# State-space layer in chunks of four steps, computed inside the input product of the second block

## The reference, cut to what matters

```
h = rms_norm(x);  proj = h @ w_in            # 1024 -> 512 u, 3*1024 qkv, 8 f, 2*1024 gates
# 32 groups of 16 channels, 64 complex states each, one step size per group
lam  = exp(a*step);  xr + i xi = B' u_t      # B' folds (lam-1)/a into b
s_t  = lam * s_(t-1) + x_t                   # over the 512 tokens
y_t  = Re(C s_t) + d*u_t;  y = gelu(y)
val, gate = split(y @ w_glu);  y_ssm = val*sigmoid(gate)
y_att = forgetting_attention(q, k, v, f)
merged = sigmoid(g_ssm)*y_ssm + sigmoid(g_att)*y_att
x = x + merged @ w_out                       # then a product-key expert layer (PEER)
```

## Time and profile before

| | us |
|---|---|
| median of 3 runs (4550.99 to 4552.28) | 4551.06 |
| the profiled execution, its own time | 4546.91 |
| its span (first to last instruction) | 4545.2 |
| in it: ada stage, up to its last bias add | 112.0 |
| in-product of block 2, first product to the next stage's first DMA | 2051.9 to 2309.8 |
| state-space stage | 2435.7 to 2729.1 |
| gated product | 2729.1 to 2799.0 |
| share of the span: PE 85%, PEld 67%, DVE 61%, ACT 40%, POOL 7% | |

### The profile page before, as it was taken

The page is one execution under the profiler, slowest core; times in us unless marked ns, Lnnn a source line. Parts: engine busy times, 40 slices in busy tenths (PEclk is TensorE's granted clock), DMA queues, the critical chain, the costliest instruction groups (busy, mean ns, idle before and its releaser), DMA issues. The chain is left out here.

```text
span 4545.2 us, 49456 instructions
## 1 busy us (share of the span) xinstructions
PE 3885.0 (85%) x17136; PEld 3062.3 (67%) x17136; DVE 2775.7 (61%) x3805; ACT 1834.6 (40%) x1841; POOL 295.8 (7%) x405
## 2 busy tenths in 40 slices
PE   7878737999999999939974437799999999999999
PEld 3656536777777777727853115678888888888887
DVE  1333538999999999952237984267787643444443
ACT  0323315777777777722233003223444443222222
POOL 0012010000000000010024420000000000000000
PEclk9875858999999999969967668899999999999999
DMA  6200118999999999962200002234444445555554
GB/s 268 97 21 0 38 55 323 358 361 359 362 356 365 359 359 363 359 223 87 87 2 10 19 9 74 79 123 160 151 177 162 168 169 206 188 190 189 187 186 143
DMA packets 212075, 840.11 MB, mean 185 GB/s; under 512 B 18672, under 2 KB 84720, under 8 KB 134160
## 3 DMA queue, kind: packets, MB, share of 16 engines
q1 hardware_dynamic: 195024, 753.53, 45.9%
q10 hardware_dynamic: 9216, 58.72, 3.1%
q0 software_dynamic: 7712, 26.23, 1.8%
HBM read 741.91 MB, written 96.50 MB: 184 GB/s over the span
## 5 line engine op out<-in xcount | busy, mean ns | idle before, releaser
L1121 DVE TENSOR_TENSOR w_low<-w_raw,w_high 128x2048 fp32r<-128x2048 f32 x399 | 909.1, 2290 | 141.9 <-ACT w_high L1050 139.5
L1050 ACT ACTIVATE w_high<-w_raw 128x2048 fp32r<-128x2048 f32 x399 | 764.6, 1916 | 336.8 <-PE ps L122 189.8
L2006 DVE TENSOR_TENSOR uv_lo<-uv_raw,uv_hi 128x2048 fp32r<-128x2048 f32 x128 | 293.5, 2293 | 662.1 <-ACT uv_hi L1863 661.8
L120 PE MATMUL ps<-w_high,xT_high 128*128 128x512 f32 x1056 | 433.1, 410 | 20.5 <-issue 20.5
L121 PE MATMUL ps<-w_low,xT_high 128*128 128x512 f32 x1056 | 417.9, 396 | 0.0
L122 PE MATMUL ps<-w_high,xT_low 128*128 128x512 f32 x1056 | 417.7, 396 | 0.0
L120 PE MATMUL ps<-h4T_high,uv_hi 128*128 128x512 f32 x1024 | 410.3, 401 | 1.1 <-DVE uv_lo L2006 1.1
L120 PE MATMUL ps<-uv_hi,w_hi 128*128 128x512 f32 x1024 | 405.1, 396 | 2.6 <-issue 2.6
L121 PE MATMUL ps<-uv_lo,w_hi 128*128 128x512 f32 x1024 | 405.0, 396 | 0.0
L122 PE MATMUL ps<-uv_hi,w_lo 128*128 128x512 f32 x1024 | 405.0, 395 | 0.0
L122 PE MATMUL ps<-h4T_high,uv_lo 128*128 128x512 f32 x1024 | 399.4, 390 | 0.0
(11 more groups left out here) (452 smaller groups left out, 6895.1 us busy)
## 6 DMA issues: line engine op xcount, KB each, us to landing
w_raw<-in_w_gate_up SPq DMA_DIRECT2D x267, 1024.0 KB, 6.9
w_raw<-in_w_down SPq DMA_DIRECT2D x132, 1024.0 KB, 6.8
uv_raw<-in_peer_u SPq DMA_DIRECT2D x64, 1024.0 KB, 5.0
uv_raw<-in_peer_v SPq DMA_DIRECT2D x64, 1024.0 KB, 5.0
a_rows<-a_out SPq DMA_DIRECT2D x128, 256.0 KB, 2.1
g_rows<-spread ACTq DMA_DIRECT2D x16, 2048.0 KB, 6.4
qT<-g_rows SPq DMA_DIRECT2D x32, 1024.0 KB, 9.0
qT<-a_rows SPq DMA_DIRECT2D x64, 512.0 KB, 8.7
```

The source lines that it names most:

```text
L120: pe.matmul(out, l_hi, r_hi, start=first, stop=False)
L1050: act.activation(w_hi[:, n % SPLIT, :], w_raw[:, n % RAW, :], ACT.Copy).then_inc(s_wh, 1)
L1121: dve.tensor_tensor(w_lo[:, n % SPLIT, :], w_raw[:, n % RAW, :], w_hi[:, n % SPLIT, :].bitcast(F32), ALU.subtract).then_inc(s_wl, 1)
L2006: dve.tensor_tensor(uv_lo[:, n % 2, :], uv_raw[:, n % 2, :], uv_hi[:, n % 2, :].bitcast(F32), ALU.subtract).then_inc(s_lo, 1)
```

## The change

Four parts.

1. Tables in the first stage. The ada stage also loads the state-space parameters (behind the first `w_ada` tile; b and c as 1 MB, d as 64 KB), and VectorE makes from them powers of lambda, b and c times powers (`b_powers`, `c_powers`) and rotation tables for 128 chunks (`turns`). TensorE turns the b tables (32 transposes after tile 3) and makes the lag kernels (32 small matmuls after tile 6). SP stores the tables to DRAM at the end: d_b, d_c, d_turn with 2 MB each (d_c in 512-byte pieces), d_lag with 0.46 MB. The loops over tiles are written out; four banks instead of three; TensorE needs no bank count for the first four tiles.
2. Chunks of four. The 512 tokens are 128 chunks of 4. A pair of groups has 4*32 = 128 input rows (step, channel), one column per chunk; scans run over 128 columns instead of 512. What happens inside a chunk is one 128x128 matmul with the lag kernels. u is multiplied out with tokens of stride 4 as the stationary operand.
3. In-product in units. The `Gemm` is replaced by 53 units: u (4), f (1), gates (16), GLU (8), qkv (24). A unit holds a depth of 256 (512 KB; f is one unit), in a ring of 3. State-space pieces lie between units; tables come by POOL's DMA queue. Gates get their sigmoid when the bank is emptied. The GLU product reads y split in high and low.
4. The state-space and GLU stages are gone. The sum with the attention's result moves to the front of mix2 (`merge`), where TensorE starts its transposes when the first half of the columns is ready.

```diff
@@ first stage @@
+            sp.dma_start(wbuf[0], ...)                      # tile 0, then parameters
+            sp.dma_start(pc[A_RE], ...)   # A_IM, LS x2
+            sp.dma_start(bc_in[...], t["ssm_bc_2"]).then_inc(s_sin, 16)
+            sp.dma_start(d_in[:, :, :], t["ssm_d_2"]).then_inc(s_sin, 16)
+            for s in range(1, RING): ...                    # tiles 1, 2, then mod, x
+            for n in range(RING, 12):
+                sp.wait_ge(s_mm_a, n - RING + 1)
+                sp.dma_start(wbuf[n % RING], t["w_ada"][n, :, :])...
+            sp.wait_ge(s_blh, 8)
+            sp.dma_start(d_b..., b_turned...).then_inc(s_prep, 16)
+            for q in range(4): sp.dma_start(d_c[q, :, :]..., c_pow[...])...
+            sp.wait_ge(s_lagd, 1);  sp.dma_start(d_lag, lags...)
+            sp.wait_ge(s_rott, 1);  # two DMAs d_turn <- turn_t
+            sp.wait_ge(s_prep, 16 * 8)
@@ its VectorE order @@
+            b_powers(0); add_bias(0); b_powers(1); add_bias(1)
+            c_first(); c_powers(0); add_bias(2); c_powers(1); add_bias(3)
+            for k in range(8): powers(k)
+            add_bias(4)
+            for k in range(5): turns(k)
+            add_bias(5); turns(5); add_bias(6); turns(6); add_bias(7)
...
@@ its TensorE @@
+            for n in range(12):
+                pe.wait_ge(s_ld_a[n % RING], (n // RING + 1) * 16)
+                if n >= BANKS_A:
+                    pe.wait_ge(s_bank_a, n - BANKS_A + 1)
...
+                if n == 3:  # 8 x 4 transposes, each 4 wait s_lb 2 and s_blh
+                if n == 6:  # wait s_el 2; 16 pairs x 2 matmuls, N = 128
@@ in-product @@
+    DEEP, UK = 3, 2
+    CHUNKS = ["u", "f"] + ["g"] * 4 + ["z"] * 4 + ["p"] * 6
+    S0 = F_END + 2
+    INPUTS_AT = {F_END + 1: 0, S0 + 1: 1, S0 + 4: 2, S0 + 6: 3}
+    OUTPUTS_AT = {S0 + 3: 0, S0 + 6: 1, S0 + 8: 2, S0 + 11: 3}
...
+                if x >= DEEP:
+                    sp.wait_ge(s_low, x - DEEP + 1)          # SP: load unit x
...
+                        if kind == "u":
+                            l = [h[:, k, :].rearrange("p (c s) -> p s c", s=SUB)[:, m, :] for h in h3T]
...
+            for x in range(NU):                              # TensorE
+                unit(x)
+                if x == F_END: turn_u()                      # 16 transposes
+                if x in INPUTS_AT: inputs(INPUTS_AT[x])      # 8 matmuls N=128
+                if x - 1 in OUTPUTS_AT: turn_y(...)          # 4 transposes
+                if x in OUTPUTS_AT: outputs(OUTPUTS_AT[x])   # 12 matmuls N=128
...
+            for x in range(NU):                              # VectorE
+                if x + 2 < NU: low(x + 2)
+                if S0 <= x < S0 + 10:
+                    next(pieces[2 * (x - S0)]);  next(pieces[2 * (x - S0) + 1])
...
@@ mix2 @@
+    def merge(dve):
+        for c in range(2):
             for m in range(TT):
+                at = merged[:, m, c * CH:(c + 1) * CH]
+                dve_steps(dve.tensor_tensor(at, at, ug[:, m, D + c * CH:D + (c + 1) * CH], ALU.mult))
+                dve_steps(dve.tensor_tensor(at, at, ug[:, m, c * CH:(c + 1) * CH], ALU.add))
+            dve.sem_inc(s_mg, 1)
```

More of the change, by code:

```diff
@@ L221, in products, with turn @@
             self.each(pe, body)
-    def turn(pe, src, s_done, s_taken, kt=KT, banks=(4, 5), at=0):
+    def turn(pe, src, s_done, s_taken, kt=KT, banks=(4, 5), at=0, ready=None):
         for k in range(kt):
+            if ready is not None and k % 4 == 0:
+                pe.wait_ge(ready, k // 4 + 1)
             if k >= 2:
@@ L483, in _ @@
[L483 to L488, removed]
+            dve.wait_ge(s_pa, 1)
+            st(dve.tensor_tensor(pc[T1], pc[A_RE], pc[STEP], ALU.mult))
+            dve.sem_inc(s_pd, 1)
+            st(dve.tensor_tensor(pc[TH], pc[A_IM], pc[STEP], ALU.mult))
@@ new lines, in _ @@
+            for k in range(5):
+                turns(k)
+            add_bias(5)
+            dve.wait_ge(s_lbt, 8)
+            st(dve.memset(lags[:, :, 0:SUB - 1, :], 0.0))
+            turns(5)
+            add_bias(6)
+            turns(6)
+            dve.sem_inc(s_rott, 1)
+            add_bias(7)
+            dve.wait_ge(s_lagh, 4)
+            dve.tensor_tensor(lags[:, :, SUB - 1, :], lags[:, :, SUB - 1, :], d_in[:, :, :], ALU.add).then_inc(s_lagd, 1)
+            for n in range(8, 12):
+                add_bias(n)
@@ L1261, in emit @@
     gain3 = sb(stage, "gain3", [P, D])
[L1262 to L1267 removed]
+    DEEP, UK = 3, 2
+    w_raw = sb(stage, "win_raw", [P, DEEP, UK * CH])
@@ new lines, in emit @@
+    w_hi, w_lo = (sb(stage, f"win_{x}", [P, DEEP, UK * CH], F32R) for x in ("high", "low"))
+    yT_hi, yT_lo = (sb(stage, f"yT_{x}", [P, 4, SEQ], F32R) for x in ("high", "low"))
+    early, late = merged[:, 0:2, :].rearrange("p m d -> p (m d)"), merged[:, 2:4, :].rearrange("p m d -> p (m d)")
+    u_rows = early.rearrange("p (n s w) -> p n s w", n=PAIRS, s=SUB)
+    y_rows2 = early.rearrange("p (s d) -> p s d", s=SUB)
+    u_sub = late.rearrange("p (n k) -> p n k", n=PAIRS)
+    flat = qkv[:, :, :].rearrange("p m d -> p (m d)")
@@ new lines, in emit @@
+    NU = len(units)
+    last_of = {at: x for x, (at, *_, last) in enumerate(units) if last}
+    U_END, F_END, G0, Z0, Q0 = last_of[0], last_of[1], last_of[1] + 1, last_of[5] + 1, last_of[9] + 1
+    s_ss, s_sq, s_root, s_g, s_h, s_tp, s_tpe, s_tph = (
+        sem(f"norm3_{x}") for x in ("sums", "mean", "root", "gain", "h", "turned", "taken", "turned_high"))
+    s_wld = [sem(f"win_ld{s}") for s in range(DEEP)]
+    s_high, s_low, s_used, s_mm, s_bank = (sem(f"win_{x}") for x in ("split_high", "split_low", "used", "mm", "bank"))
@@ new lines, in emit, with wait_used @@
+    s_tb, s_tt, s_tc = ([sem(f"ssm_{x}_table{s}") for s in range(2)] for x in ("b", "turn", "c"))
+    s_u, s_uh, s_v, s_vu, s_z, s_y, s_yh, s_yt, s_yhi, s_ylo, s_gl = (
+        sem(f"ssm_{x}") for x in ("u_turned", "u_here", "inputs", "inputs_used", "states", "y", "y_here", "y_turned", "y_high", "y_low",
+                                  "gated"))
+    used_before = [sum(not u[-1] for u in units[:x + 1]) for x in range(NU)]
+    def wait_used(eng, x):
+        if units[x][-1]:
+            eng.wait_ge(s_mm, 4 * (units[x][0] + 1))
+        else:
+            eng.wait_ge(s_used, used_before[x])
```

737 lines of the change are left out of this document (464 added, 273 removed).

## The result

The changed kernel takes 4277.64 us (median of 4 runs, 4272.19 to 4278.32), the kernel before 4551.02 us beside it (median of 4). The ratio is 0.9401, 95% interval 0.9390 to 0.9412. The forecast was 4276, with a range of 4256 to 4312. The profiled execution took 4272.19 us; the forecast of that was 4272.3. That the two are so close is partly luck: single terms were off by up to 3.5 us, in both directions, and the profiled execution was the fastest of the four.

A forecast was written before the change was run, and what follows sets the result against it. VectorE was taken to bound the state-space stage, TensorE the in-product. Terms -363.3 + 69.9 + 9.8 + 9 = -274.6 from 4546.9 give 4272.3, plus 4.2 for the median: 4276 us, range 4256 to 4312.

The forecast's parts named there:

- What bounds what: VectorE sets the state-space stage's length, TensorE the in-product's; work moved there costs only what it costs TensorE.
- Stages removed, -363.3: State-space and GLU stages, from the first's first DMA to mix2's first DMA, drop out: -363.3 us.
- In-product, forecast +69.9: In-product stage grows by 43.5 + 25 + 3 - 2.0 + 0.4 = +69.9 us.
- The GLU's 192 products: In the in-product, 192 GLU matmuls of 512 columns at 0.2267 us each add +43.5 us.
- State space: TensorE's state-space passes and transposes in the in-product add +25 us, bounds 21 to 28.
- f in the middle, +3: In-product's f chunk behind u: following work starts at the low clock, +3 us, bounds -9 to +6.
- Strided loads, 0 taken: In-product, u's 96 stride-4 weight loads stay hidden, 0 us; rival at 0.44 adds 20 us, chance 0.10.
- Start, -2.0: In-product's start: VectorE splits two half-size units before turning to h, -2.0 us.
- What has to stay hidden: In-product: VectorE's 56 us fit beside 54 of products plus some 20 of passes; leak rival 4320, chance 0.14.
- mix2, +9.8: Front of mix2: 16 merges, 11.6 us, now precede the first `turned_low`, adding +9.8 us.
- First stage, forecast +9: First stage ends at 121 instead of 112 us, set by table stores: +9, bounds 0 to +20.
- The step from the profiled execution to the median: Whole kernel: the median of the runs lies 4.2 us above the profiled execution, added at the end.

The follow-up runs named there:

- experiment 2: Changed kernel without VectorE's state-space arithmetic inside the in-product, semaphores still raised at the same places: 4276.27 us.
- experiment 3: Changed kernel without any state-space work in the in-product (TensorE, ScalarE, VectorE, table loads); gated product reads the normed input instead: 4252.32 us.
- Experiment 1: Kernel before the change with its state-space and GLU stages left out, nothing else changed: 4182.7 us, ratio 0.9189.
- experiment 5: Changed kernel with the f chunk's operands swapped, 24 products of 512 columns plus four transposes in place of 96 of 8: 4260.51 us, ratio 0.9368.
- experiment 6: Changed kernel with the first stage's table stores moved to ScalarE's queue, each as soon as its table is done: 4271.73 us, ratio 0.9383.
- experiment 7: Changed kernel with the first stage's load of x moved behind that of tile 3: 4272.59 us, ratio 0.9388.
- 8: Changed kernel with mix2's first low parts of the turned operand made between the merges of the second half: 4273.42 us, ratio 0.9391.
- 10: Changed kernel with mix2's first four low parts between the merges and the first weight tile's split early: 4272.53 us, ratio 0.9397.
- experiment 9: Changed kernel with stationary tokens at stride four in f, q, k, v and stride two in the gates: 4285.33 us.
- experiment 4: Changed kernel with 9 of VectorE's 512-column instructions and 8 scans issued once more per state-space quarter: 4299.93 us.
- experiment 11: Changed kernel with f's operands swapped, table stores early, x behind tile 3, and mix2's merges woven with its first split early: 4250.32 us, ratio 0.9341.

## Why the prediction was right, step by step

- **What bounds what.** VectorE set the state-space stage and TensorE the in-product; work moved under TensorE then costs TensorE's part alone. Shown by experiments 2 (38.7 us of VectorE, no time) and 3.
- **Stages removed, -363.3.** Experiment 1 gave 363.6.
- **In-product, forecast +69.9, measured +67.6.** The GLU's 192 products at 0.2267 stand as forecast (43.5; 1184 to 1376 instructions, and no waits). State space: 25 forecast, 23.2 measured (experiment 3). Of these, 1.7 are there because u's transposes run at the low clock, which the forecast counts under f, so 21.5 stand against the 25. The pass was put too near its upper bound of 0.144, a row that holds the drain of a chain: 16 input passes took 1.70 us from start to start, 0.106 each.
  The parts as measured: 43.5 + 23.2 + 1.1 (restart behind f) + 0.7 (u's loads) - 2.7 + 1.4 (start) + 0.4 (end, taken over from the forecast and not measured) = 67.6; measured 67.6.
- **f in the middle, +3.** The chunk took 16.14 us, as before (16.1 by its starts), and the clock fell once, as forecast. The restart cost 1.1 (five products, 2.24 us in place of 1.13), the slower transposes 3.33 - 1.67 = 1.7 (experiment 5), 2.8 in all. Part of it is luck: in five other runs with this chunk unchanged (3, 6, 7, 8 and 10) the clock fell 2.8 to 3.0 us after its start and it took 17.65 to 17.8, while u had fewer products at the low clock. What I did not see is that the chunk's 16 us could be had for 5.5; it was read as a given.
- **Strided loads, 0 taken.** 0.7 measured; "a load of twice that still hides" was right but for 0.0083 each. The Trainium skill (SBUF — State Buffer, section "SBUF: two separate sides") says that each element at this stride touches a new 16-byte line; the bare load of 0.2335 against 0.111 agrees with its direction, and at stride 2, where two elements share a line, this case shows a price as well (0.0068), which the rule doesn't lead one to expect.
- **Start, -2.0.** The first product came 2.7 us earlier after the stage's first DMA (23.50 instead of 26.17), but 14 products ran at the low clock where it had been 7, which is 1.4 us back. That number varies from run to run with the same code ahead (7 in experiments 3 and 5, 1 in experiment 9).
- **What has to stay hidden.** Forecast was 56 us of VectorE against 54 of products and some 20 of passes; measured were 55.1 busy in 71. The Trainium skill (same page and section) has the rule that VectorE instructions of a two-port kind shut out GpSimd's writing of descriptors. This case shows no such effect: the tables' loads landed a median of 6.7 to 7.7 us after issue, and 6.5 to 8.1 in experiment 2, where VectorE does none of the state space; no TensorE wait names them.
- **mix2, +9.8.** From mix2's first DMA to the first split on VectorE it took 21.65 us, before 11.39: +10.3. From that DMA to the end of the program it was +8.8 in this execution; the seven others with the same code had +8.7 to +13.6.
- **First stage, forecast +9, measured +11.9.** The gap was where it should be (8.1 us for 6.7 forecast, tile 3 at 41.7 for 39), TensorE done at 118.2 for 117. The term that was mis-sized is the stores. They started 3 us sooner than forecast, at 98, but ended at 124 instead of 121: 26 us from first issue to the end, where 20 were forecast. The forecast reckoned with 2 MB in 4.9 us, 428 GB/s, and 2 us extra for the c powers in pieces of 512 bytes. From 98 to 122.5 us the DMA engines were busy nearly throughout (mean share 1.01, the last tile's load among it) but moved 349 GB/s. The four issues of the c powers also kept SP's queue for 14.9 us, and the turns were issued behind them at 115. No run changes the size of the pieces, so what this queue and what the slower transfer cost each isn't shown. Experiments 6 and 7 show the two halves of the stage: the stores set the end, and x in front of tile 3 the gap.

The mechanism held: what was removed, what was hidden and what TensorE paid came out as forecast. That the sum fits to 0.2 us is luck. The errors of +2.9 (first stage) and -2.3 (in-product), with +1.0 (attention), -0.8 (blocks between) and -1.0 (mix2), took each other away, in an execution whose first stage and whose end were among the shortest of those with the same code. The step from the profiled execution to the median was forecast as 4.2 us and was 5.5. The total should be read as right to some 3 us.

## What to carry to other kernels

Here the work of an engine with room cost nothing inside a stage that another engine fills, and some 20 us more of it would still have been covered. What decides is its busy time in the very stretch against the length of the stretch (here 55 in 71, with splits two units ahead), not the mean of the stage. When small pieces are moved, look at what they do to the clock of what follows, and at whether they must be small: swapping the stationary and the moving operand gave 14 us, where moving the chunk had cost 2.8. And a store whose results are needed much later can leave when its table is ready, on a queue that nothing urgent uses: that gave 3.6 us in experiment 6.

## What the hardware showed that was not expected

- Gaps cost more than their length here. Three waits of 17.9 us together lengthened a stage by 24.7 (experiment 4). After 8.1 to 8.3 us without work TensorE's next 16 products took 8.8 to 10.1 us in nine runs; after 3.0 us they took 7.13 in one run (experiment 7) and after 3.1 us 8.83 in another (experiment 11).
- The clock also fell under full load: 42 products of 8 columns ran 0.11 apart, then the granted clock went to 1.2 GHz and they were 0.21 apart, with no idle time between. In other runs of the same code it fell 26 to 42 products after the start. With 512 columns moving in the same place it stayed at 2.4 GHz (experiment 5).
- Four DMA issues of 512 KB, in pieces of 512 bytes, took 0.6 to 9.6 us each on SP's queue, 14.9 in all; the 2 MB store ahead of them took 0.4. The DMA engines were busy meanwhile, so this is no price of an issue on idle engines.
- The load of a stationary operand at a stride of 16 bytes with its small product takes 0.2335 us, at either clock. Behind a product of 512 columns it shows as 0.0083, at a stride of 8 bytes as 0.0068 (experiment 9).
